# The attention value product turned over, one head of a pair after the other

## The reference, cut to what matters

```python
p = masked_softmax(logits, mask, sink)                    # (heads, query, key)
o = jnp.einsum('bgrts,bsgd->btgrd', p, vb)                # value product, head size d = 64
...
o_b = gb[..., 0, :] * o_cmp + gb[..., 1, :] * o_sel + gb[..., 2, :] * o_win
y = jnp.concatenate([o_a * jax.nn.silu(z_a), o_b * jax.nn.silu(z_b)], axis=-1)
out = y.astype(x.dtype) @ w_out
```

## Time and profile before

| | |
|---|---|
| median of 3 runs | 1460.82 us (1460.75 to 1461.81) |
| span of the profiled execution | 1460.2 us |
| attention steps | 204.9 to about 317.2 us of the span |
| first full unit of the output projection starts | about 325.0 us |
| PE busy over the span | 98% |
| PE busy, 205.0 to 224.9 us | 17.54 of 19.90 us |

### The profile page before, as it was taken

One profiled execution on the slowest core, in us unless ns is written; L12 is line 12 of the kernel. 1 busy time (PEld: TensorE's weight loads), 2 busy tenths in 40 slices (PEclk: granted clock), 3 DMA queues, 4 the chain that ended last, 5 costly groups with the idle time before them and its releaser, 6 DMA issues.

```text
span 1460.2 us, 18290 instructions
## 1 busy us (share of the span) xinstructions
PE 1436.3 (98%) x6990; PEld 1207.1 (83%) x6990; DVE 741.5 (51%) x1200; ACT 601.3 (41%) x1009; POOL 112.4 (8%) x131
## 2 busy tenths in 40 slices
PE   6999999999999999999999999999999999999998
PEld 5788879998888888888888888888888888888887
DVE  6741677855665533556455444453457333333332
ACT  5633577755343332333333444532355333333221
POOL 5302322210000000000000111100000000000000
PEclk9999999999999999999999999999999999999999
DMA  9995200123433333312223233344332333333321
GB/s 283 322 237 186 75 1 2 31 73 93 152 101 109 98 97 101 101 44 87 68 63 87 58 87 101 87 144 113 89 90 84 115 89 101 99 93 94 110 79 57
DMA packets 227825, 149.71 MB, mean 103 GB/s; under 512 B 5330, under 2 KB 216014, under 8 KB 227108
## 3 DMA queue, kind: packets, MB, share of 16 engines
q1 hardware_dynamic: 223588, 131.63, 31.2%
q0 software_dynamic: 4160, 17.04, 4.0%
HBM read 140.92 MB, written 6.68 MB: 101 GB/s over the span
## 4 chain that ended last, share of the span: by engine, by line
PE 95%; SPq 1%; DMA 1%; DVE 1%; ACT 1%; issue 1%; DVEq 0%; ACTq 0%
PE ps L433 70%; PE ps L2215 6%; PE ps L2241 3%; PE ps L1938 3%; PE ps L2140 3%; PE ps L1830 3%; PE ps L2227 1%; DMA w_raw<-in_w_in_dram 1%; PE ps L1961 1%; PE ps L1899 1%; PE ps L2126 1%; PE ps L2125 1%; SPq L547 1%; PE ps L1954 1%; SPq L577 0%
## 5 line engine op out<-in xcount | busy, mean ns | idle before, releaser
L453 DVE TENSOR_TENSOR w_lo<-w_raw,w_hi 128x1024 fp32r<-128x1024 f32 (+1 forms) x214 | 258.1, 1209 | 251.0 <-ACT w_hi L448 248.1
L448 ACT ACTIVATE w_hi<-w_raw 128x1024 fp32r<-128x1024 f32 (+1 forms) x214 | 219.4, 1034 | 15.3 <-PE ps L433 11.3
L499 ACT ACTIVATE temps<-ps 128x512 f32<-128x512 f32 x67 | 40.0, 597 | 238.9 <-PE ps L433 238.9
L433 PE MATMUL ps<-g_hi,w_hi 128*128 128x512 f32 x384 | 95.8, 392 | 0.0
L433 PE MATMUL ps<-g_hi,w_lo 128*128 128x512 f32 x384 | 94.9, 389 | 0.0
L433 PE MATMUL ps<-g_lo,w_hi 128*128 128x512 f32 x384 | 94.8, 389 | 0.0
L433 PEld LDWEIGHTS ps<-g_hi,w_lo 128*128 128x128 f32 x384 | 72.1, 188 | 15.0
L433 PEld LDWEIGHTS ps<-g_lo,w_hi 128*128 128x128 f32 x384 | 72.1, 188 | 14.9
L433 PEld LDWEIGHTS ps<-g_hi,w_hi 128*128 128x128 f32 x384 | 71.5, 188 | 14.6
L433 PE MATMUL ps<-f_lo,w_hi 128*128 128x512 f32 x288 | 71.1, 389 | 0.0
L433 PE MATMUL ps<-f_hi,w_hi 128*128 128x512 f32 x288 | 71.1, 389 | 0.0
(11 more groups left out here) (442 smaller groups left out, 2734.8 us busy)
## 6 DMA issues: line engine op xcount, KB each, us to landing
w_raw<-in_w_in_dram SPq DMA_DIRECT2D x107, 512.0 KB, 3.9
w_raw<-in_w_ff_gate_dram SPq DMA_DIRECT2D x22, 512.0 KB, 3.8
w_raw<-in_w_ff_up_dram SPq DMA_DIRECT2D x22, 512.0 KB, 3.8
w_ada_shift_scale<-in_w_ada_dram SPq DMA_DIRECT2D x16, 512.0 KB, 7.8
w_raw<-in_w_r_out_dram SPq DMA_DIRECT2D x16, 512.0 KB, 4.5
w_raw<-in_w_ff_down_dram SPq DMA_DIRECT2D x16, 512.0 KB, 4.2
w_ada_gate<-in_w_ada_dram SPq DMA_DIRECT2D x4, 1024.0 KB, 10.9
x_spill<-x_t POOLq DMA_DIRECT2D x2, 2048.0 KB, 9.0
```

The costliest lines, as they stand in the source:

```text
L433: mm = pe.matmul(bank, w[:, slot, k], mov[:, at_k], start=first and n == 0 and k == 0, stop=last and n == 2 and k == kts - 1)
L448: act.activation(whi[:, slot, 0:kts], raw[:, slot, 0:kts], ACT.Copy).then_inc(hi_done, 1)
L453: nc.vector.tensor_tensor(wlo[:, slot, 0:kts], raw[:, slot, 0:kts], whi[:, slot, 0:kts].bitcast(F32), ALU.subtract).then_inc(lo_done, 1)
L499: act.activation(dst, ps[:, o % 4], func, scale=scale).then_inc(evac, 1)
```

## The change: what it does

**The value product is turned.** The 64 columns of values are now the stationary operand and the transposed probabilities are streamed, 128 columns. The head's 64 numbers come out on 64 partitions: the even step of a pair on partitions 0 to 63, the odd one on 64 to 127, tokens along the free axis. So heads 2k and 2k+1 fill one 128 by 128 tile of the bank (`weighted`). All key blocks of the even head are followed by all those of the odd one. The order of heads within a group becomes 0 to 7.

**Steps go in pairs.** In iteration n, PE scores steps 2n and 2n+1, then weighs pair n-2, then transposes the two steps of pair n-1. There are four score buffers and four `probs_t` buffers; two of the latter lie in the weight slot of the last projection unit, so SP holds back output unit 3 until all value products are done.

**The coefficients become a tile.** 1/row sum times gate is one number per token and head, and tokens are now on the free axis. POOL widens the coefficients of each group to 128 by 512 (`widen`), PE transposes them (four transposes, `coefficients_wide`), ACT copies them to SBUF (`coef_wide`), and DVE multiplies bank and tile (`combined`). That is 12 groups of four transposes. The 8 groups of four transposes of out_a and out_b fall away. The multiplication with silu(z) goes from DVE to POOL (`y_gate`), but for the last half, where DVE puts silu(z) into the coefficients.

**The compressed branch.** Its coefficients are multiplied into the probabilities by POOL before their transposes, which move from ahead of step 0 into iteration 3; the four products move to iterations 5, 7, 9 and 11.

```diff
-CONVERT_AT = 61
-CO_PE_AT = ((0,), (2, 4), (10, 12), (16, 18))
-CO_AT = (2, 6, 14, 20)
-K_WINDOW_AT = (4, 6, 8, 9)
+CONVERT_AT = 31
+CTR_AT = 3
+CO_PE_AT = (5, 7, 9, 11)
+K_WINDOW_AT = (2, 3, 4, 4)
+Y_AT = (15, 19, 22, 31, 34, 43, 46, 49)
...
@@ SP
             for k in range(KT):
+                if k == 3:
+                    sp.wait_ge(m["pv_mm"], PAIRS)
                 load(None, 0, U_WO + k, w_out_v[:, :, k * P:(k + 1) * P])
...
@@ POOL
-            for b in (1, 2):
-                for part in range(4):
-                    k_rest(b, part)
+            for part in range(4):
+                k_rest(1, part)
+            pool.wait_ge(m["csoft_done"], 3)
...
+            g.tensor_tensor(csc_heads, csc_heads,
+                            cden[:].rearrange("p g q -> p (g q)").unsqueeze(2).to_broadcast([P, 32, NC_PAD]),
+                            ALU.mult).then_inc(m["cpool_done"], 1)
+            pool.wait_ge(m["cpool_done"], 2)
+            for part in range(4):
+                k_rest(2, part)
...
+            def widen(G):
+                pool.wait_ge(m["cf_done"], G + 1)
...
+                g.tensor_copy(wide_of(G).rearrange("p t (h d) -> p t h d", h=2),
+                              coef[:, G % 2].rearrange("p (t h) -> p t h", h=2).unsqueeze(3).to_broadcast([P, 4, 2, HD])
+                              ).then_inc(m["cpool_done"], 1)
+            for G in range(2):
+                widen(G)
+            for i in range(NI - 1):
+                if i:
+                    y_gate(i, 0)
+                    widen(3 * i + 1)
                     y_rest(i, 0)
                 add_branch(i, 1)
+                widen(3 * i + 2)
+                if i == 0:
+                    y_gate(i, 0)
+                add_branch(i, 2)
+                if i == 0:
+                    y_rest(i, 0)
+                y_gate(i, 1)
+                widen(3 * i + 3)
+                y_rest(i, 1)
...
@@ ACT, iteration n
+                if n == CTR_AT + 1:
+                    act.wait_ge(m["aux_tr"], 1)
+                    a.activation(cpt[:, 0], ps[:, 6], ACT.Copy).then_inc(m["aux_ev"], 1)
...
+                G = (n - 7) // 4
+                if n >= 7 and (n - 7) % 4 == 0 and G < N_GROUPS - 1:
+                    act.wait_ge(m["aux_tr"], G + 3)
...
+                    a.activation(coef_wide(G), ps[:, 6], ACT.Copy).then_inc(m["aux_ev"], 1)
...
@@ DVE
+            def combined(G):
...
+                if G == N_GROUPS - 1:
+                    gated = coef_wide(G).rearrange("p (t n) -> p t n", t=4)
+                    v.tensor_tensor(gated, ps[:, 6].rearrange("p (t n) -> p t n", t=4),
+                                    proj[:, ZB:ZB + 4, (NI - 1) * P:S], ALU.mult).then_inc(m["aux_ev"], 1)
...
+                v.tensor_tensor(dst[:], ps[:, 4 + G % 2], coef_wide(G), ALU.mult).then_inc(m["comb_done"], 1)
...
@@ PE
-                    for b in range(blocks):
-                        c = (u.first_block + b) * P + u.g * HD
-                        mm = pe.matmul(ps[:, 4 + u.group % 2, u.head * HD:(u.head + 1) * HD], pt[:, t % 2, blk(b)],
-                                       proj[:, v, c:c + HD], start=b == 0, stop=b == blocks - 1)
-                    mm.then_inc(m["pv_mm"], 1)
...
+            def weighted(n):
+                u = att(2 * n)
+                pe.wait_ge(m["pt_d"], n + 1)
+                pe.wait_ge(m["pt_a"], n + 1)
...
+                for half in range(2):
                     for b in range(blocks):
                         c = (u.first_block + b) * P + u.g * HD
+                        mm = pe.matmul(ps[half * HD:half * HD + HD, 4 + u.group % 2, blk(n % 4)], proj[:, v, c:c + HD],
+                                       pt_of(2 * n + half)[:, blk(b)], start=b == 0, stop=b == blocks - 1)
+                mm.then_inc(m["pv_mm"], 1)
+            def coefficients_wide(G):
+                pe.wait_ge(m["cpool_done"], G + 3)
...
+                for t in range(4):
+                    mm = trans(ps[:, 6, blk(t)], wide_of(G)[:, t])
+                mm.then_inc(m["aux_tr"], 1)
+            for n in range(PAIRS + 1):
+                if n < PAIRS:
+                    scored(2 * n)
+                    scored(2 * n + 1)
+                if n == 0:
+                    v_local()
+                if n >= 2:
+                    weighted(n - 2)
+                if n >= 1:
+                    transposed(2 * n - 2)
+                    transposed(2 * n - 1)
+                if n == CTR_AT:
+                    compressed_transposed()
+                if n in CO_PE_AT:
+                    compressed_out(CO_PE_AT.index(n))
+                if n >= 6 and (n - 6) % 4 == 0:
+                    coefficients_wide((n - 6) // 4)
+            early_out(0)
+            weighted(PAIRS - 1)
+            coefficients_wide(N_GROUPS - 1)
```

More of the change, by code:

```diff
@@ L141, in att @@
     return Step(s)
-def tails_at(s):
-    return [(i, half) for i in range(NI) for half in range(2)
-            if s == (24 * i + 29 + 3 * half if i < NI - 1 else 24 * i + 13 + 17 * half)]
 class Own:
@@ L1014, in _ @@
[L1014 removed]
+                    a.activation(pt_of(t)[:, 0:w], ps[:, 3, 0:w], ACT.Copy).then_inc(m["pt_a"], 1)
+                if n == CONVERT_AT:
                     act_convert(act, None, 0, U_LAST + AHEAD)
[L1016 to L1019 removed]
+                for part, k in enumerate(K_WINDOW_AT):
+                    if n == k:
+                        k_round(2, part)
@@ L1507, in _ @@
[L1507 to L1513 removed]
+                    v.tensor_copy(pt_of(t)[:, 0:w], ps[:, 2, 0:w]).then_inc(m["pt_d"], 1)
@@ new lines, in _ @@
+                if n == PAIRS:
+                    coefficients(N_GROUPS - 1)
+                if n >= 7 and (n - 7) % 4 == 0 and n < PAIRS:
+                    combined((n - 7) // 4)
+            combined(N_GROUPS - 1)
+            i, rows = NI - 1, slice(4, 8)
+            dve.wait_ge(m["ob_done"], 2 * NI)
+            dve.wait_ge(m["comb_done"], N_GROUPS)
+            dve.wait_ge(m["yl_done"], 2 * i)
+            v.tensor_tensor(y_f[:, 1], o_tmp[:].rearrange("p (t n) -> p t n", t=4),
+                            ob[:, i].rearrange("p (t n) -> p t n", t=4), ALU.add).then_inc(m["yf_done"], 1)
```

420 lines of the change are left out of this document (210 added, 210 removed).

## The result

The changed kernel takes 1481.98 us (median of 4 runs, 1480.95 to 1482.38) against 1460.78 us for the kernel before on the same chip (1460.58 to 1461.81). The ratio is 1.0141, with a 95% interval of 1.0126 to 1.0155: 21.2 us slower, where 10.8 were forecast. The profiled runs have spans of 1478.4 and 1460.2 us, so 18.2 us can be placed in the trace. The changed kernel's other three runs had spans 2 us above its profiled one, at mean granted clocks of 0.992 to 0.993 where the profiled one has 0.994: the profiled run is its mildest.

What follows compares the result with a forecast made beforehand. PE was taken to bound the kernel, busy for 98% of the span. Terms for passes, overlap, switches, early pairs, clock, coefficients, slack and tail summed to +10.8 us on 1460.2, plus 0.6: 1471.6 us, range 1455 to 1482.

Steps and rivals of the forecast that it cites:

- Value passes: Turned value product on PE: 432 passes stay at 0.107 us each, no gain and no loss.
- Overlap: Two heads in different column halves of PE's array: one pass per pair runs alongside, 36 pairs, -3.9 us.
- Switches: PE's array going into and out of the 64-column tile: 0.25 us per round trip, +9.0 us in 36 pairs.
- Coefficients against output transposes: Late attention and tail: two more groups of four PE transposes, +0.9 us; ACT's extra copies and POOL's gating fit.
- Slack: Late stretch: transposes follow exponentials by one and a half pairs, so half of 3 us of small waits go, -1.5 us.
- (a): Early pairs: PE waits 0.5 us for POOL's scaling of the compressed probabilities, counted as 2.5 us long.
- (b): Iteration 5: PE's compressed product waits 1.0 us for ACT's copy of the compressed transposes.
- (c): End of iteration 6: PE's first coefficient transposes wait 2.1 us for POOL's first widening, queued behind products, remainders and band copies.
- Side by side throughout: Rival: value passes of the two heads share the array throughout, 20.5 us go in late pairs, 1455.0 us; chance 0.13.
- Cheap switches: Rival: a switch costs what the 32-column product shows or less and the heads overlap, 1459 to 1465 us; chance 0.22.
- no load ahead: Rival: a 64-column load no longer hides behind the pass before, 384 passes add 20.4 us, 1492 us; chance 0.07.
- The early stretch decides: Rival: longer waits in the first 12 pairs with the clock down again, up to 5 us more, 1476 us; chance 0.10.

Runs made afterwards that it cites:

- experiment 3: Changed kernel with the value product loading 128 stationary columns, so no small tile or switch (first head's output overwritten, timing only): 1486.61 us.
- Experiment 6: Changed kernel with DVE's coefficient multiplication one pair later and ACT's exponential waiting only until DVE has read the denominators: 1480.92 us.
- experiment 4: Changed kernel with POOL widening the first coefficients ahead of its two band copies instead of behind them: 1479.08 us.
- experiment 2: Changed kernel with the value product's key blocks as outer loop and the two heads in turn inside: 1475.89 us.
- experiments 1: Changed kernel with DVE's coefficient multiplication called one pair later, ACT's exponential still waiting for the multiplication two groups before: 1507.96 us.
- experiment 8: Changed kernel with heads in turn, first widening ahead of the band copies, and later multiplication with ACT's nearer wait, all together: 1470.21 us.
- experiment 5: Changed kernel with each pair's value product and transposes split by head and interleaved, so twice the array switches: 1503.62 us.

## Why the prediction was right in direction and short in size

1471.6 us were forecast, with a range of 1455 to 1482; 1481.98 came, at the range's very end. The direction was right, but that the time stayed in the range was partly luck: the late waits cost 12 us more than I gave them, and the overlap, worth 11 us more than I gave it, made up for most of that. With the overlap as small as forecast it would have been some 1493 us. In the trace, against the span:

| term | forecast us | measured us |
|---|---|---|
| value passes, 36 late pairs | 0 | +3.3 |
| overlap, 36 late pairs | -3.9 | -15.3 |
| switches, 36 late pairs | +9.0 | +10.4 |
| early stretch, first switches included, without the clock | +4.7 | +4.6 |
| clock | +0.8 | +1.7 |
| coefficients, slack and waits of the late stretch | +0.9 - 1.5 | +11.6 |
| tail | +0.8 | +1.4 |
| elsewhere | 0 | +0.5 |

The late waits are what is left of 10.0 us when the first three rows are taken off.

**Value passes (forecast 0).** Nearly right. Against the earlier trace rows the full array of experiment 3 needs 3.58 us for a pair at 512 keys, 2.69 at 384 and 1.81 at 256, where before it was 3.48, 2.60 and 1.72. So the new shape with no switch and no overlap costs 0.09 to 0.10 us per pair whatever the number of passes, some 3.3 us in 36 pairs. My reading of why it goes by the pair is that one pass of each set was short before: in the step of the earlier trace rows the first value pass takes 0.055 us to the next and the other seven 0.11, and the weight load of that first one starts at 300.93 us, with the score product ahead of it still running. In experiment 3, where each pass streams 128 columns, the first one takes 0.11 us like the rest. A pair had two such sets, so it loses 2 x 0.055 us. My mean of 0.107 us hid that.

**Overlap (forecast -3.9).** Under-sized. I let one pass per pair overlap. Against experiment 3 the changed kernel's pairs are 0.12, 0.11 and 0.15 us shorter at 512, 384 and 256 keys; with the switch's 0.29 added back, the overlap is 0.41, 0.40 and 0.44 us, which is four passes each time, as the starts of the single passes show. In turn it is 3.58 - 2.97 + 0.29 = 0.90 us at 512 keys and 2.69 - 2.31 + 0.29 = 0.67 at 384: 8 and 6 passes, which is every pass of the second head. I wrote that eight passes of one half stand in the queue ahead of the other's, and that is what the order decides: head after head only the last four passes of the first head have company, and with two key blocks (four passes) that is all there is, which is why the order made no difference there. Why it is four, at every width, no run shows. In 36 pairs (20, 8 and 8 of 256, 384 and 512 keys) the term was 20 x 0.44 + 8 x 0.40 + 8 x 0.41 = 15.3 us, not 3.9. The Trainium skill, TensorEngine Tiling (Array Packing), section When to Use Tiling, counts a doubling for 64 stationary columns; the trace agrees for the heads in turn (two passes in each 0.11 us; 1.02 us with the way out, against 1.78 with the full array) and not for head after head (1.51 us).

**Switches (forecast 0.25 us each, +9.0).** Near: 0.29 us, as read from experiment 3, so 10.4 us in 36 pairs. The bracketing by three small rows, with the value between them, held, though its upper end came from a wrong reading: by its own rule the last full pass of the earlier trace rows starts at 197.03 + 2.09 - 0.39 = 198.73 us and not at 198.62, which makes that way in 0.11 us and the end 0.25, not 0.36. The Trainium skill, TensorEngine Tiling (Array Packing), section Key Properties, says that a change of mode drains the engine; the trace agrees, and puts this figure on it.

Together the three came to about 3.3 - 15.3 + 10.4 = -1.6 us in 36 pairs, where I had +5.1; the undisturbed pairs themselves say the same (3.46, 2.58 and 1.65 us against 3.48, 2.60 and 1.72). By these alone the kernel would have been a little faster than before.

**Coefficients against output transposes (forecast +0.9).** This is the step that failed. I counted 0.9 us for the extra transposes, wrote that ACT's copies of 0.58 us "fit", and named POOL's `widen(3)` as the tightest place. I judged ACT by its busy share, and did not ask who waits for the copy: DVE's multiplication, with the next pair's row minima queued behind it. It happens in nearly every group of four pairs. Experiment 6 removed it and took 4.75 us from the stretch. That is the part of the 11.6 us that an experiment shows. What is left, 87.87 us, is still 3.5 us above before, and 5.2 us with the clock's 1.7 us taken off the kernel before: 0.9 for the transposes, and 5.1 more of PE's waits than before (6.0 against 0.9: for ACT's copies 3.0 us, for POOL at iteration 18 1.3 us, and 1.7 us with no releaser in the profile), less the 1.6 us above, which leaves some 0.8 us without a place. That split is read from the waits, not tested.

**Slack (forecast -1.5).** It did not come. My reading, which no run tests, is that pairs in place of steps leave more time to each exponential, but the work that falls once per group then delays a whole pair.

**The early waits (forecast 0.5 + 1.0 + 2.1).** (a) did not exist: POOL's product took 1.91 us, not 2.5, and started at 208.67 us. In its place PE waited 1.18 us, up to 207.99 us, for row minima behind DVE's gating, which I had moved with the rest and given no duration. (b) was 0.89 us. (c) was 2.96 us, for the cause named, and experiment 4 confirms it: the band copies ahead of the widening are worth 2.0 us in the trace and 2.9 in the median. In all 5.0 us of waiting for 3.6. That the whole early stretch without the clock came to 4.6 us for a forecast of 4.7 (1.5 + 3.2) is luck in part, as one of the three waits was another than the one forecast.

**The clock (forecast +0.8).** It cost 1.7 us more than before, inside the forecast's ends of 0 and 3. PE was busy for 1.01 of 2.00 us from 207 us on, where the mean clock was 0.71, and from 209 us it was at 0.50, the 1.2 GHz level. The direction was right, the size twofold. I had put the cost before at 1 us, as I had read only the first of two windows; it was 1.7. With the 3.4 us of the clock the early stretch came to 8.0 us for a forecast of 5.5.

**The tail (forecast +0.8).** It was +1.4: PE waited 0.90 us for DVE's last remainder (1.1 forecast), and 0.78 us at 330.07 for a copy of probabilities, which I did not see.

**The rivals.** Side by side throughout is what experiment 2 does in the pairs themselves; 6.1 us were to be had by it, not the 16.6 between it and my forecast (20.5 - 3.9), since the changed kernel already had 15.3 of them. I had written that this rival decides as soon as more than three passes per pair overlap. Four did, so its mechanism came three quarters true, and the time still went the other way, by the waits. Cheap switches and no load ahead are both refuted, by the 0.29 us read from experiment 3 and by value passes 0.109 us apart with loads of 64 columns. The early stretch decides holds for little: 2.5 us beyond my sum came from there, but all of it is the clock, and the kernel before lost 1.7 us of that too, only later.

The numbers to be looked for read as follows. The holes were 0.09 us on either side, just under the 0.1 I looked for and over the 0.05 that would have told against me. Value passes are 0.086 us apart on the mean of both heads ((1.58 - 0.285)/15), but those of one head are 0.109 us apart, so the sign of being wrong that I had named, passes of one head closer than 0.09, did not come. Two starts close together came once per pair (0.006 us), but behind them three more passes of the second head lay between those of the first. PE did wait for POOL's coefficient tile, up to 222.98 us and not near 217. Step 24 came at 232.97, not 228, and the full output unit at 342.55, not 336.

## What to carry to other kernels

Where a kernel is bound by one engine, price a moved instruction by its place in each queue, not by the busy share of the engine that runs it: here a copy of 0.58 us on an engine with time to spare held a multiplication on another engine, and through it the scores behind it, in nearly every group. Two products in different column halves of the array run side by side only as far as the order of issue lets them, so alternate them block by block. And when a wait is moved, list who waits on the semaphore it signals: experiments 1 and 6 differ only in which of DVE's two signals ACT waits for, by 27 us, more than half of which is the clock that fell after the waits. And compare stretches of two kernels only after the granted clock of each has been looked up: the 84.33 us that the late stretch took before hold 1.7 us of it.

## What the runs showed of the hardware that was not expected

**Small vector operations that last as long as POOL's.** In the changed kernel's timeline:

```profile
211.39 1.26 POOL L768 TENSOR_TENSOR w_lo<-proj,w_hi 64x512 fp32r<-64x512 f32 x1 [0.80 <-POOL compressed_probs L818]
...
211.60 1.07 DVE L1528 TENSOR_TENSOR sink_arg<-row_min,sinks_negated 128x8 f32<-128x8 f32 x1
```

Eight elements per partition take 1.07 us, ending at 212.67, 0.02 us after POOL's operation (212.65). The gating addition of 1.15 us ends at 206.98, where POOL's operation ends at 206.91; a multiplication of 128x8 that takes 0.86 us ends at 333.94, POOL's at 333.91. With POOL idle the same multiplication took 0.17 us in experiment 8, and the gating addition took 0.20 us in the kernel before, where it began 0.07 us ahead of POOL's operation (which still took its usual 1.26 us). Reciprocals are not held: one of 128x8 took 0.19 us at 332.85 in the middle of a POOL operation. The Trainium skill, SBUF — State Buffer, section SBUF: two separate sides, says that the two engines share one pair of ports, that some forms of VectorE's operations take it as an exclusive lock, and that the first to start holds it for its whole instruction; the three long durations, each begun behind a POOL operation, and the short ones of the multiplication and the addition agree with it; that POOL's operation was not held in its turn does not show it. No run here moved POOL's work away from the gating, so the cause is read from the ends and not tested.

**Column halves overlap in full when they alternate.** The second head's eight passes at 512 keys cost nothing in turn (1.02 us for 16 passes, and 1.02 us for the eight of one head alone in experiment 5). Head after head, four passes overlap at 256, 384 and 512 keys alike.

**A first pass at half the price.** With 128 stationary and 64 streamed columns the first value pass behind a score product takes 0.055 us and each further one 0.11.

**The clock early in the attention differs from run to run.** From 205 to 233 us the mean clock was 0.88 in the changed kernel's profiled run and 0.76 in that of experiment 6, whose program is the same up to iteration 7. A saving of a microsecond in that stretch can't be read from one profile.
